# Modulation strips summed on VectorE, and gate and up products of two feed-forward layers with both halves of the split tokens as 512 moving columns

## The reference, cut to what matters

```
# FFN1 (first block): conv_glu
a = h @ w_gate;  u = h @ w_up
y = (gelu(conv3(a)) * u) @ w_down          # widths 1024 -> 2816 -> 1024

# FFN2 and FFN3 (second block): swiglu, once before and once after its attention
y = (silu(h @ w1) * (h @ w3)) @ w2         # widths 1024 -> 2816 -> 1024

# modulation of the second block
mod = silu(c) @ ada_w + ada_b              # 1024 -> 9216, for one row c
```

## Time and profile before

| | |
|---|---|
| median of 3 runs | 1079.49 us (1078.52 to 1080.01) |
| profiled execution | 1079.18 us |
| its span, first to last instruction | 1077.4 us |
| mean granted clock of TensorE | 0.992 of 2.4 GHz |
| PE busy | 1033.9 us of the span |
| DVE busy | 759.1 us |
| ACT busy | 508.6 us |
| matmuls | 7757 rows |

### The profile page before, as it was taken

One profiled execution on the slowest core, in us unless ns is written; L12 is line 12 of the kernel. 1 busy time (PEld: TensorE's weight loads), 2 busy tenths in 40 slices (PEclk: granted clock), 3 DMA queues, 4 the chain that ended last, 5 costly groups with the idle time before them and its releaser, 6 DMA issues.

```text
span 1077.4 us, 19131 instructions
## 1 busy us (share of the span) xinstructions
PE 1033.9 (96%) x7757; PEld 973.7 (90%) x7757; DVE 759.1 (70%) x1116; ACT 508.6 (47%) x608; POOL 2.1 (0%) x5
## 2 busy tenths in 40 slices
PE   6999999999999999999999999999979899999998
PEld 5999768899999999899999989978867899999997
...
GB/s 226 245 145 157 79 78 90 145 229 277 234 233 239 230 181 271 105 342 276 308 271 311 266 145 163 183 118 79 118 40 78 157 195 217 224 185 195 186 165 39
DMA packets 163149, 200.03 MB, mean 186 GB/s; under 512 B 13216, under 2 KB 138138, under 8 KB 163098
## 3 DMA queue, kind: packets, MB, share of 16 engines
...
HBM read 198.25 MB, written 1.05 MB: 185 GB/s over the span
## 4 chain that ended last, share of the span: by engine, by line
PE 82%; DVE 9%; ACT 6%; issue 2%; DMA 1%; SPq 0%; DVEq 0%; ACTq 0%
PE psX L1632 15%; PE psX L1633 15%; PE psX L1634 15%; PE psA L1632 5%; PE psA L1634 5%; PE psA L1633 5%; DVE wlo L924 2%; PE psX L1670 2%; PE psX L1671 2%; PE psA L1639 2%; PE psA L1640 2%; PE psA L1641 2%; PE psX L1680 1%; ACT whi L494 1%; PE psX L1945 1%
## 5 line engine op out<-in xcount | busy, mean ns | idle before, releaser
L924 DVE TENSOR_TENSOR wlo<-raw,whi 128x2048 fp32r<-128x2048 f32 x151 | 346.4, 2295 | 153.0 <-ACT whi L494 152.8
L494 ACT CAST whi<-raw 128x2048 fp32r<-128x2048 f32 x150 | 285.3, 1906 | 293.7 <-PE psX L1634 177.1
L1632 PE MATMUL psX<-hh,whi 128*128 128x256 f32 x1400 | 403.4, 288 | 3.2 <-DVE wlo L924 1.9
L1633 PE MATMUL psX<-hl,whi 128*128 128x256 f32 x1400 | 396.6, 283 | 0.0
L1634 PE MATMUL psX<-hh,wlo 128*128 128x256 f32 x1400 | 396.6, 283 | 0.0
L1632 PEld LDWEIGHTS psX<-hh,whi 128*128 128x128 f32 x1400 | 269.1, 192 | 8.8 <-issue 6.7
L1633 PEld LDWEIGHTS psX<-hl,whi 128*128 128x128 f32 x1400 | 269.2, 192 | 2.2 <-issue 1.7
L1634 PEld LDWEIGHTS psX<-hh,wlo 128*128 128x128 f32 x1400 | 269.0, 192 | 0.0
L1632 PE MATMUL psA<-oh,whi 128*128 128x256 f32 x384 | 111.2, 289 | 1.6 <-DVE ol L1484 1.6
L1262 DVE SCALAR_TENSOR_TENSOR adacc<-scr,small,adacc 128x256 f32<-128x256 f32 (+1 forms) x175 | 105.3, 602 | 5.8
L1633 PE MATMUL psA<-ol,whi 128*128 128x256 f32 x384 | 108.6, 283 | 0.0
...
## 6 DMA issues: line engine op xcount, KB each, us to landing
...
```

The source lines that it names most:

```text
L494: a_.copy(whi[b % 3][:, :], raw[b % 3][:, :]).then_inc(sem("hi_ready"), 1)
L924: v_.tensor_tensor(wlo[b % 3][:, :], raw[b % 3][:, :], whi[b % 3][:, :].bitcast(F32), ALU.subtract).then_inc(sem("lo_ready"), 1)
L1632: pe.matmul(dst, wh, xh, start=start, stop=False, skip_group_check=True)
L1633: pe.matmul(dst, wh, xl, start=False, stop=False, skip_group_check=True)
```

## The change

Two things are changed.

- **The products.** `hh` and `hl` become the two halves of one buffer `hhl` (k, 2, 256). In FFN2 and FFN3 `wide` replaces `gemm` for the gate and up chunks of the loop: one matmul with whi has hh and hl side by side as 512 moving columns, and its result stands in one PSUM bank, the high product in columns 0 to 255 and the low product in 256 to 511; a second matmul adds hh with wlo to columns 0 to 255. Gate takes banks 0 and 1 of `psX`, up banks 2 and 3. The first pair (`wide_pair`) keeps 256 columns but writes to the same places. The halves are now added outside PE: ACT copies the low half of the gate to `f_t` (`low_gate`) and of the up to `f_u` (`low_up`), DVE adds the high half of the gate (`gate_sum`, before the silu) and of the up (in `hidden`, before the product).
- **The modulation.** After each `ada_piece` DVE transposes `adacc` in 32 x 32 blocks and reduces over 32 columns into `ada_parts`. `ada_fold` replaces `ada_sums`: four float32 matmuls once a layer, with a 128 x 32 matrix `fold` as weights and 22, 44 or 6 moving columns: in down(10) of FFN1 and FFN2 and before down(9) of FFN3. In FFN3 the bias, the halving and the diagonal matrices for the output gate (L1346 before) move on DVE from before the last step to behind it.

```diff
+    part("fold")[p, p % 32] = 1.0
...
-        hh = sb("hh", [KT, S], F32R)
-        hl = sb("hl", [KT, S], F32R)
+        hhl = sb("hhl", [KT, 2, S], F32R)
+        hh, hl = hhl[:, :, 0, :], hhl[:, :, 1, :]
...
+        f_u = ksum[:, 0:2, :]
...
+        ada_t, ada_parts = take(512), take(4 * 72)
...
+                        act.wait_ge(sem("gsum_ready"), FSTEP * (f - 1) + i + 1)
+                    a_.activation(f_g, f_t, ACT.Gelu if f == 0 else ACT.Silu).then_inc(sem("ge_ready"), 1)
+
+                def low_gate(i):
+
+                    if f:
                         act.wait_ge(sem("wt_used"), b + 3 * i + (1 if isinstance(i, int) and i == 0 else 0))
-                    a_.activation(f_g, f_t if f == 0 else psW[:, 0, :].rearrange("p (a s) -> p a s", a=2),
-                                  ACT.Gelu if f == 0 else ACT.Silu).then_inc(sem("ge_ready"), 1)
+                        a_.copy(f_t, psX[:, 0:2, S:2 * S]).then_inc(sem("low_gate"), 1)
+
+                def low_up(i):
+
+                    if f:
+                        act.wait_ge(sem("wt_used"), b + 3 * i + (2 if isinstance(i, int) and i == 0 else 1))
+                        a_.copy(f_u, psX[:, 2:4, S:2 * S]).then_inc(sem("low_up"), 1)
...
+                    act.wait_ge(sem("actf_ready"), FSTEP * f + i + 1)
+                    low_gate(i + 1)
                     hi(b + 5, i)
-                    act.wait_ge(sem("actf_ready"), FSTEP * f + i + 1)
                     gate(i + 1)
+                    low_up(i + 1)
...
-                dve.wait_ge(sem("ada_sum"), pieces)
-                link(v_.tensor_tensor(modT[:, c0:c1], psS[:, 256 + c0:256 + c1], colB("ada_b", c0, c1 - c0), ALU.add))
+                dve.wait_ge(sem("ada_fold"), pieces)
+                src = psS if c1 < 72 else psX[:, 0, :]
+                link(v_.tensor_tensor(modT[:, c0:c1], src[:, 256 + c0:256 + c1], colB("ada_b", c0, c1 - c0), ALU.add))
...
+            def gate_sum(f, nb_, i, first):
+
+                dve.wait_ge(sem("low_gate"), FSTEP * (f - 1) + 1 + i + first)
+                v_.tensor_tensor(f_t, psX[:, 0:2, 0:S], f_t, ALU.add).then_inc(sem("gsum_ready"), 1)
...
+                if r or ks == KT:
+                    n = 2048 // ks
+                    dve.wait_ge(sem(f"ada{r}_used"), (group if r else u) + 1)
+                    link(v_.transpose(ada_t[:, 0:n], acc))
+                    c0 = 88 + 16 * group if r else 8 * u + (88 if isinstance(u, int) and u >= 2 * FSTEP else 0)
+                    dst = ada_parts[:, c0:c0 + n // 32] if isinstance(c0, int) else ada_parts[:, bass.ds(c0, n // 32)]
+                    v_.tensor_reduce(dst, ada_t[:, 0:n].rearrange("p (b k) -> p b k", k=32), AXX, ALU.add).then_inc(sem("ada_part"), 1)
...
-                v_.tensor_tensor(f_a, f_g, upp, ALU.mult).then_inc(sem("actf_ready"), 1)
+                if f:
+                    dve.wait_ge(sem("low_up"), FSTEP * (f - 1) + 1 + i + first)
+                    link(v_.tensor_tensor(f_a, psX[:, 2:4, 0:S], f_u, ALU.add))
+                v_.tensor_tensor(f_a, f_g, f_a if f else upp, ALU.mult).then_inc(sem("actf_ready"), 1)
...
-                if f == 0:
-                    conv(f, b + 2, i, 1)
+                (gate_sum if f else conv)(f, b + 2, i, 1)
...
+                step(f, b, FSTEP - 2)
                 if f == 2:
                     half_gate(f)
                     for k in range(KT):
                         v_.tensor_scalar(gdiag[:, k // 4, P * (k % 4):P * (k % 4) + P], ident, modT[:, 64 + k:65 + k], None,
                                          ALU.mult).then_inc(sem("gate_diag"), 1)
-                step(f, b, FSTEP - 2)
...
+            def wide_pair(b, m, second):
+
+                for n in range(2):
+                    if n:
+                        second()
+                    have(b + n)
+                    wh, wl = (kview(x, KT) for x in (whi[(b + n) % 3], wlo[(b + n) % 3]))
+                    for k in range(KT):
+                        if n == 0:
+                            pe.wait_ge(sem("hhi_ready"), KT * m + k + 1)
+                        for t in range(2):
+                            dst = psX[:, 2 * n + t, 0:S]
+                            pe.matmul(dst, wh[:, k, P * t:P * t + P], hh[:, k, :], start=(k == 0), stop=False, skip_group_check=True)
+                            pe.matmul(dst, wl[:, k, P * t:P * t + P], hh[:, k, :], start=False, stop=(k == KT - 1), skip_group_check=True)
+                for n in range(2):
+                    wh = kview(whi[(b + n) % 3], KT)
+                    for k in range(KT):
+                        if n == 0:
+                            pe.wait_ge(sem("hlo_ready"), KT * m + k + 1)
+                        for t in range(2):
+                            ins = pe.matmul(psX[:, 2 * n + t, S:2 * S], wh[:, k, P * t:P * t + P], hl[:, k, :],
+                                            start=False, stop=(k == KT - 1), skip_group_check=True)
+                    ins.then_inc(sem("wt_used"), 1)
+
+            def wide(b, n, i):
+
+                have(b, i)
+                wh, wl = (kview(x[b % 3], KT) for x in (whi, wlo))
+                for t in range(2):
+                    bank = psX[:, 2 * n + t, :]
+                    for k in range(KT):
+                        pe.matmul(bank, wh[:, k, P * t:P * t + P], hhl[:, k, :, :].rearrange("p a s -> p (a s)"),
+                                  start=(k == 0), stop=(k == KT - 1), skip_group_check=True)
+                        ins = pe.matmul(bank[:, 0:S], wl[:, k, P * t:P * t + P], hh[:, k, :], start=False, stop=(k == KT - 1),
+                                        skip_group_check=True)
+                ins.then_inc(sem("wt_used"), 1)
...
-            def ada_sums(f, i):
-
-                if f == 1:
-                    pe.wait_ge(sem("ada1_used"), i + 1)
-                else:
-                    pe.wait_ge(sem("ada0_used"), f * FSTEP + i + 1)
-                n = 4 if f == 1 else 2
-                c0 = 256 + n * i + MOD_AT[f]
-                for k in range(n):
-                    dst = psS[:, c0 + k:c0 + k + 1] if isinstance(i, int) else psS[:, bass.ds(c0 + k, 1)]
-                    ins = pe.matmul(dst, adacc[:, P * k:P * k + P], ones[:, 0:1], start=True, stop=True,
-                                    skip_group_check=True)
-                ins.then_inc(sem("ada_sum"), 1)
+            def ada_fold(f):
+
+                pe.wait_ge(sem("ada_part"), (FSTEP, 2 * FSTEP, 2 * FSTEP + ADA_TAIL)[f])
+                c0, c1 = MOD_AT[f], MOD_AT[f + 1]
+                for q in range(4):
+                    ins = pe.matmul((psX[:, 0, :] if f == 2 else psS)[32 * q:32 * q + 32, 256 + c0:256 + c1], cst("fold"), ada_parts[:, 4 * c0 + q:4 * c1:4],
+                                    start=True, stop=True, skip_group_check=True)
+                ins.then_inc(sem("ada_fold"), 1)
 
             def ffn(b, f, m, acc_free):
...
                 if f == 2:
-                    gemm_pair(b, [psW[:, 0, :], psW[:, 1, :]], m, 0)
+                    wide_pair(b, m, lambda: None)
                 pe.wait_ge(sem(acc_free[0]), acc_free[1])
                 for a in range(4):
                     pe.matmul(psA[:, a, :], zeros[:, :], zeros[:, 0:1].broadcast_to([P, 512]), start=True, stop=False, skip_group_check=True)
-                if f < 2:
+                if f == 0:
                     gemm_pair(b, [psW[:, 0, :], psW[:, 1, :]], m, 0)
                 if f == 1:
-                    pe.wait_ge(sem("final_ready"), 1)
+                    wide_pair(b, m, lambda: pe.wait_ge(sem("final_ready"), 1))
 
                 def step(i):
 
-                    pe.wait_ge(sem("ge_ready" if f else "conv_ready"), FSTEP * f + i + 1)
-                    gemm(b + 2, psW[:, 0, :], hh, hl, i)
-                    if f == 1:
-                        ada_sums(f, i)
+                    if f:
+                        pe.wait_ge(sem("gsum_ready"), FSTEP * (f - 1) + i + 1)
+                        wide(b + 2, 0, i)
+                    else:
+                        pe.wait_ge(sem("conv_ready"), i + 1)
+                        gemm(b + 2, psW[:, 0, :], hh, hl, i)
                     pe.wait_ge(sem("actf_ready"), FSTEP * f + i + 1)
-                    gemm(b + 3, psW[:, 1, :], hh, hl, i)
-                    if f == 0 or (f == 2 and isinstance(i, int) and i < ADA_TAIL):
-                        ada_sums(f, i)
+                    if f:
+                        wide(b + 3, 1, i)
+                    else:
+                        gemm(b + 3, psW[:, 1, :], hh, hl, i)
+                    if f == 2 and isinstance(i, int) and i == FSTEP - 2:
+                        pe.wait_ge(sem("gsum_ready"), 2 * FSTEP)
+                        ada_fold(f)
...
-                    if o == 1 and f < 2:
-                        ada_sums(f, FSTEP - 1)
+                    if o == 2 - f:
+                        ada_fold(f)
```

18 lines of the change are left out of this document (10 added, 8 removed).

## The result

The changed kernel takes 1073.58 us (median of 7 runs, 1071.78 to 1076.58) against 1079.6 for the kernel before beside it (7 runs, 1078.52 to 1082.29): ratio 0.9944, 95% interval 0.9929 to 0.9959. The profiled execution took 1073.02. The forecast was 1065.0 (1058 to 1071): the direction was right, the gain less than half of what was forecast, and the time outside the range.

A forecast was written before the change was run, and what follows sets the result against it. PE was taken as the bound, busy 1033.9 of 1077.4 us; -2.8 in FFN1, -8.5 in FFN2 and -2.9 in FFN3 sum to -14.2 us from the profiled 1079.18, giving 1065.0 us, with 80 in 100 between 1058 and 1071.

The forecast's parts named there:

- A wide chunk is 16 x (0.227 + 0.120) = 5.55 us: Gate and up chunks on PE in FFN2 and FFN3: 5.55 us in place of 5.76, 0.21 saved each.
- a rival of 0.05 with 1072.6: Wide chunks in FFN2 and FFN3: a 512-column matmul costs its two halves, 0.240 us, giving 1072.6; chance 0.05.
- The end keeps its length: FFN1's end: unchanged, as the fold, longer than the last sum by 0.45, lies ahead of an existing wait.
- The fold: Four float32 matmuls on PE once a layer, priced 0.9 us each, 2.7 in all.
- the pair: Each strip's transposition and reduction on DVE: delays what follows by 1.45 us in FFN2, 0.91 in FFN1 and FFN3.
- -2.8: FFN1's whole change in us: down(9) at 380.22, where ada_sums stood at 382.98, with the end unchanged.
- FFN2's start: FFN2 up to down(0): starts at 463.2 against 463.13 before, so all that the first step saves is lost.
- Its end, 13.2 us after down(9): FFN2's end: first mean 13.2 us after down(9) starts, against 10.0 before, +3.2 us.
- DVE's step 16.4: FFN2's steps: DVE busy 16.4 us, under PE's 16.86 by 0.46, so PE sets the pace.
- Neither DVE nor the loads bound the steps: FFN2's steps, two rivals: DVE binds (1069 to 1078, chance 0.11); loads bind at 18.1 us (1076.5, chance 0.03).
- the rival asked for 0.022: Wide chunks: weight load uncovered by over 0.022 us per k-tile and column tile cancels the gain; chance 0.03.
- Its 8.4 us for the products: FFN2 and FFN3 on PE: 40 wide chunks saving 0.21 us each, 8.4 us in all.

The follow-up runs named there:

- k8: The changed kernel run again with nothing altered; 1072.8 us, ratio 0.9938.
- k2: The changed kernel with each strip's transposition and reduction on DVE replaced by two small copies, the sum over partitions left out; 1067.27 us, ratio 0.9885.
- k13: The kernel before run again with nothing altered; 1080.97 us.
- k14: The kernel before run a third time with nothing altered; 1081.4 us.
- k10: The changed kernel with wide matmuls grouped by width, narrow first gate and up, and the next layer's low part behind the fourth x addition; 1061.94 us.
- k5: The changed kernel with the next layer's first low part on DVE behind the fourth addition to x at FFN1's and FFN2's ends; 1068.98 us.
- k11: k10 with FFN2's fold issued behind the fourth group of the last down product instead of the first; 1062.01 us, ratio 0.9816.
- k6: The kernel before with only the modulation strips changed (k1), plus k5's move of the low part at the ends; 1065.72 us, ratio 0.9874.
- k12: k10 with eight matmuls of zeros on PE ahead of FFN2's fold; 1061.96 us, ratio 0.9825.
- k7: The changed kernel with each FFN2 strip transposed twice, 0.74 us more DVE work a step; 1078.71 us, ratio 0.9994.
- k1: The kernel before with only the modulation strips moved to DVE, gate and up products left at 256 columns; 1072.15 us, ratio 0.9932.

## Why the prediction was wrong

- **"A wide chunk is 16 x (0.227 + 0.120) = 5.55 us"**: this term was mis-sized. It is 5.65, a saving of 0.11 a chunk and not 0.21. The steps are 17.07 us in FFN2 and 16.79 in FFN3, where 16.86 and 16.54 were forecast: 9 x 0.21 + 9 x 0.25 = 4.1 us, of which the cheaper fold gives 0.6 back. The prediction had the bound (0.240) and priced it as a rival of 0.05 with 1072.6; the truth lies between. The row it went by was of runs of one width, the tokens standing and the weights moving. The Trainium skill's 2.5 ns a matmul ("TensorE: Matmul & The Clock Gate", "Wait — 56ns, not 53.3ns?"), which the prediction cited, would give 0.04 a chunk. Grouped by width the saving is 0.18. Both 0.11 and 0.18 lie between the page's 0.04 and the forecast's 0.21, and the measurement decides.
- **"The end keeps its length"** in FFN1 failed. The fold was watched, but the pair stands on DVE ahead of the low part and of x. The end is 1.17 us longer in the profiled execution, 0.3 of it a late slice, and 0.85 in k8; without the pair (k2) it is 9.69, where it was 9.78 before. Part of this miss is hidden, because -2.8 was itself too small: it sets down(9) against the sums ahead of it, at 382.98, where down(9) itself stood 0.36 later.

```profile
383.34 0.36 PE L1632 MATMUL psA<-oh,whi 128*128 128x256 f32 x1
```

- **The sum was made as if the clock did the same.** It did not: +3.0 us ahead of FFN1 in the profiled execution, by chance (k8 has not got it, k13 and k14 have it without the change), and behind FFN2 up to 3.5 in others, 0.6 of it from the stretch near 775 us. The second seems to hang on the change, with PE's waits at FFN2's end. Sorted by how long PE stood still between down(9) and the mean, the clock was halved within that stretch or in the 15 us behind it in nine of ten traces with 2.5 us or more (the changed kernel's first, with 3.9, is the tenth), in one of the two with 2.0 to 2.3 (k10, not k5; k11, like k10 but for the fold's place, has 2.5), and in none of the five with 0.9 or less (the three of the kernel before, k6, k12). Where it was halved, a start or an end that stalls costs a second time. That PE's stillness is the cause is argued from these counts, and the wait of 2.17 us that stands behind the mean in every trace may have a part in it that no run separates; k12 fits and does not prove it.
- **The fold** takes 0.2 to 0.3 us, not 0.9. PE waits 1.97 us ahead of it in FFN2, but by k11 this wait costs nothing, since DVE's chain sets the mean.
- **What held.** FFN2's start was forecast to give back all that its first step saves: -0.11 measured. Its end, 13.2 us after down(9): 13.22. down(0) waits 1.39 us for hidden_lo in FFN2 (1.7 forecast) and 1.71 in FFN3 (1.8). DVE's step 16.4: 16.49 by k7; its lead is 0.58 where 0.46 was forecast, the larger only because PE's step is longer. The transposition 0.71 (0.69 taken), the reduction 0.69. Neither DVE nor the loads bound the steps: after the first, all of FFN2's take 17.07 us. The weight load stayed covered but for 0.006 us a pair at most, where the rival asked for 0.022.
- **What was not asked.** The prediction priced the two parts together. Its 8.4 us for the products stood beside longer starts and ends that were charged to both parts at once. k1 splits them: 4.7 of that length belongs to the products, whose steps save 3.5.
